# One stage in place of three ahead of the RWKV solve: sums over time on TensorE, two products on GpSimd

## The chip, the cores and the metric

One core of a Trainium2 chip runs the whole program. Times are device microseconds of that core; the metric is the time of one execution, and the median of three is given. The engines are TensorE (PE in the profile), VectorE (DVE), ScalarE (ACT), GpSimd (POOL) and SyncE (SP), which issues transfers.

## The reference

A model block with dilated attention beside a bidirectional RWKV-7 mixer, then a layer of retrieved experts, then a second block of four layers. What matters here is how the mixer prepares its recurrence, for 256 tokens and 8 heads of 64:

```python
zr = token_shift(z[..., 3 * A:], mu_prev, mu_next)      # r, k, v (512 each), xw, xa (64), xg (128)
g = jax.nn.sigmoid(xg) @ g_up
kk = hs(k * k_k)
kk = kk * lax.rsqrt(jnp.maximum(jnp.sum(kk * kk, axis=-1, keepdims=True), 1e-12))
for direction in range(2):
    w = -jax.nn.softplus(-(w_decay0[direction] + jnp.tanh(xw) @ w_decay_up[direction])) - 0.5
    decay = jnp.exp(-jnp.exp(w))
    a = jax.nn.sigmoid(a_gate0[direction] + xa @ a_gate_up[direction])
    k_dir = k * (1.0 + (a - 1.0) * k_a)
    ys.append(wkv7_scan(hs(r), hs(decay), hs(k_dir), hs(v), kk, hs(a), reverse=(direction == 1)))
# wkv7_scan: S_t = S_{t-1}(diag(w_t) - kk_t^T (a_t*kk_t)) + v_t^T k_t,  y_t = S_t r_t
```

The logarithm of the decay is `-exp(-0.5) * sigmoid(...)`, so decays over a stretch of tokens are exponentials of sums over time.

## The kernel before

Activations lie with features on the partitions: `zT[:, i, :]` is 128 features by 256 tokens. `rT`, `kT`, `vT` are four such tiles each; `zT[:, 20]` holds `xw` (partitions 0 to 63) and `xa` (64 to 127), `zT[:, 21]` holds `xg`. The program is a row of stages. In each, every engine has its own list of instructions, written out by hand, and waits on semaphores; a stage ends when all engines have ended it, and the next one begins some 0.3 us later. PSUM is `ps`, eight banks of 512 columns. All products here are in float32, which the trace shows as two passes for each.

The recurrence is solved in chunks of 128 tokens by matrix products (the stage that begins with line 1805). It needs, for each direction d, four factors (`alpha`, `beta`, `kappa`, `rho`), and `v`, `beta`, `kappa` turned so that tokens are on the partitions (`v_tok`, `bk_tok`). Three stages make them:

- Stage 1 (lines 1522 to 1565): TensorE multiplies `lora` by `zT[:, 20]`, 64 rows for the decay (line 1549) and the other 64 for the gate (1551). ScalarE takes tanh, then sigmoids with the bias in the instruction (`logw`, `aa`). TensorE also goes through the last eight of 32 tiles of a modulation matrix (`late_rows`, 464), which SyncE loads into a ring of six slots in `alpha`, `beta` and `kappa` (`late_load`, 429): six in the attention stage before, two here, when slots are free.
- Stage 2 (1567 to 1685): VectorE sums `logw` over time with 16 scans (1638), takes the sum at the chunk's middle off (1648), and makes the sum without the token's own term (1653). ScalarE takes three exponentials for each direction (1621 to 1623). VectorE scales `kk` (1659), makes the bonus (1663 to 1668), and multiplies ten times over 128x1024 (1671 to 1677).
- Stage 3 (1689 to 1716): TensorE turns six chunks (1700), VectorE and ScalarE copy three each.

The weights of later layers come through a ring of six slots, in order, refilled when a slot is used.

Of the kernel before, what the change touches and what calls it, by code (L numbers as in the profile page):

```python
# [30 lines left out]
P = 128  # L31
S = 256
# [20 lines left out]
ADA_LATE, LATE_RING = 32, 6  # L53
# [7 lines left out]
for _name, _n in (("c", 8), ("ada_b", 48), ("norm1_g", 8), ("mu_prev", 14), ("mu_next", 14), ("w_decay0", 8), ("a_gate0", 8),  # L61
                  ("k_k", 4), ("k_a", 4), ("r_k", 4), ("lnx_g", 4), ("lnx_b", 4), ("norm2_g", 8), ("q_norm_g", 1),
                  ("k_norm_g", 1), ("norm_w", 48), ("final", 8), ("pool_scale", 4), ("s5_d", 4), ("lam_re", S5T),
                  ("lam_im", S5T), ("log_dt", S5T)):
    VEC[_name] = (_at, _at + _n)
    _at += _n
# [79 lines left out]
def build(nc, A):  # L146

    with ExitStack() as ctx:
# [273 lines left out]
        late_in = [sem(f"late_in{i}") for i in range(LATE_RING)]  # L422
        late_used = sem("late_used")

        def late_load(sp, i):

            if i >= LATE_RING:
                sp.wait_ge(late_used, i - LATE_RING + 1)
            sp.dma_start(late_slot(i), A["ada_late"][i]).then_inc(late_in[i % LATE_RING], 16)
# [27 lines left out]
        def late_rows(pe, pair, bank):  # L457

            for n in range(2):
                i = 2 * pair + n  # L460
                pe.wait_ge(late_in[i % LATE_RING], 16 * (i // LATE_RING + 1))
# [691 lines left out]
        def attention(pairs, out, tag, late_of=None):  # L1153
# [25 lines left out]
            with ExitStack() as tmp, stage() as (block, (scored, shifted, maxed, exped, probs_ready, turned, turned_back,  # L1179
                                                         mixed, out_copied, lowered, v, *_)):  # L1180
                DEEP = 3
                if late_of:
                    @block.sync
                    def _(sp):
                        for i in late_of:
                            late_load(sp, i)
# [173 lines left out]
        def late_slot(i):  # L1360

            slot = i % LATE_RING
            return (alpha, beta, kappa)[slot // 2][:, slot % 2].rearrange("p a t -> p (a t)")
# [3 lines left out]
        lora_in = sem("lora_in")  # L1367
        attn = ExitStack()
# [132 lines left out]
        def head(tensor, i):  # L1501
# [5 lines left out]
                   for j in range(4)], mix, "dilated", range(LATE_PREP, LATE_PREP + LATE_RING))  # L1507
# [6 lines left out]

        feat = ExitStack()
        g_up = sb("g_up", [P, 512], where=feat)
        logw = sb("logw", [P, 2, 4, S], where=feat)
# [4 lines left out]
        with stage() as (block, (up_in, squashed, raised, sig_done, v, *_)):  # L1522
            @block.sync
            def _(sp):
                sp.dma_start(g_up[:, :], A["g_up"]).then_inc(up_in, 16)
                for i in range(LATE_PREP + LATE_RING, ADA_LATE):
                    late_load(sp, i)

            @block.scalar
            def _(act):  # L1530
                nc.scalar.activation(zT[0:64, 20, :], zT[0:64, 20, :], ACT.Tanh).then_inc(squashed, 1)
                nc.scalar.activation(zT[:, 21, :], zT[:, 21, :], ACT.Sigmoid).then_inc(squashed, 1)
                for d in range(2):
                    act.wait_ge(raised, 8 * d + 8)
                    for j in range(4):
                        bank, col = 4 * d + j // 2, j % 2 * S
                        nc.scalar.activation(logw[:, d, j, :], ps[:, bank, col:col + S], ACT.Sigmoid,
                                             bias=vec("w_decay0", 4 * d + j)).then_inc(sig_done, 1)
                        nc.scalar.activation(aa[:, d, j, :], ps[:, bank + 2, col:col + S], ACT.Sigmoid,
                                             bias=vec("a_gate0", 4 * d + j)).then_inc(sig_done, 1)  # L1540

            @block.tensor
            def _(pe):
                pe.wait_ge(lora_in, 16)
                pe.wait_ge(squashed, 1)
                for d in range(2):
                    for j in range(4):
                        bank, col = 4 * d + j // 2, j % 2 * S
                        nc.tensor.matmul(ps[:, bank, col:col + S], lora[0:64, d, j * P:(j + 1) * P], zT[0:64, 20, :],
                                         start=True, stop=True).then_inc(raised, 1)  # L1550
# [1966 lines left out]
```

## Time and profile before

| what | us |
|---|---|
| median of three runs | 2083.81 (2081.59 to 2084.3) |
| the profiled execution | 2085.11 |
| its span | 2083.2 |
| TensorE busy | 1839.3 (88%) |
| VectorE busy | 1488.5 (71%) |
| ScalarE busy | 1007.0 (48%) |
| GpSimd busy | 455.2 (22%) |

The shares are averages over the whole program. The change touches the stretch from 165.5 to 217.4 us, and the rows below are of that stretch and its borders. The clock column is the share of TensorE's full clock that was granted.

### The profile page before, as it was taken

How to read it: one execution, taken by the hardware profiler on the slowest of the kernel's cores; microseconds unless marked ns; L12 is line 12 of the kernel's file. 1: busy time of each engine (PE TensorE's matmuls, PEld its weight loads, DVE VectorE, ACT ScalarE, POOL GpSimd, SP SyncE). 2: the span in 40 equal slices, each digit the busy share in tenths (PEclk: the TensorE clock that was granted, in tenths of full speed). 3: DMA queues.
4: the chain of work that ended last, by engine and by line, in shares of the span. 5: the costliest groups of instructions: out<-in, count | busy, mean ns of one | idle time of the engine just before them, and what ended most of it. 6: DMA issues, size and time to landing. Idle time of an engine off the chain costs nothing. (4 is left out here: it accounts for less than half of the span.)

```text
span 2083.2 us, 33313 instructions
## 1 busy us (share of the span) xinstructions
PE 1839.3 (88%) x12202; PEld 1376.2 (66%) x12202; DVE 1488.5 (71%) x2602; ACT 1007.0 (48%) x2038; POOL 455.2 (22%) x463
## 2 busy tenths in 40 slices
PE   5974899988888777887789999889999999989998
PEld 4842887744443222222259999769998899968997
DVE  7666664787776776776567667877678887887666
ACT  3445212564444445444355555466556555546554
POOL 1010220144454433444410001002123331110000
PEclk8987999899999999999999999799999999999999
DMA  8870000499999999999965556125556556425553
GB/s 329 290 265 26 3 3 29 152 420 421 421 421 422 421 421 421 421 419 421 421 249 191 191 192 240 51 73 184 188 184 226 178 185 186 137 93 181 190 186 97
DMA packets 102973, 497.23 MB, mean 239 GB/s; under 512 B 11856, under 2 KB 16208, under 8 KB 69712
## 3 DMA queue, kind: packets, MB, share of 16 engines
q1 hardware_dynamic: 65312, 226.68, 32.4%
q0 software_dynamic: 36864, 268.45, 31.0%
q8 instruction: 67, 1.10, 0.2%
q10 hardware_dynamic: 688, 0.65, 0.1%
q14 instruction: 42, 0.34, 0.0%
HBM read 494.69 MB, written 1.05 MB: 238 GB/s over the span
## 5 line engine op out<-in xcount | busy, mean ns | idle before, releaser
L253 PE MATMUL ps<-srcs,wh 128*128 128x512 f32 x2000 | 711.7, 397 | 6.3 <-DVE srcs L267 3.4
L2267 PE MATMUL ps<-row,diag 128*128 128x512 f32 x1024 | 495.7, 619 | 118.9 <-ACT diag L2379 118.7
L255 PE MATMUL ps<-srcs,wl 128*128 128x256 f32 x2000 | 563.2, 282 | 0.0
L235 DVE TENSOR_TENSOR wl<-ring,wh 128x1024 fp32r<-128x1024 f32 x362 | 459.1, 1273 | 92.7 <-ACT wh L229 91.5
L2267 PEld LDWEIGHTS ps<-row,diag 128*128 128x128 f32 x1024 | 181.3, 192 | 421.1 <-ACT diag L2379 269.6
L2486 DVE CUSTOM_DVE_ANT_0 row<-row,h_tok 128x1024 f32<-128x1024 f32 x256 | 313.3, 1224 | 191.5 <-DMA row<-in_peer_uv,experts 181.4
L253 PEld LDWEIGHTS ps<-srcs,wh 128*128 128x128 f32 x2000 | 376.8, 188 | 93.3 <-issue 7.6
L229 ACT ACTIVATE wh<-ring 128x1024 fp32r<-128x1024 f32 x362 | 378.8, 1052 | 69.8 <-PE ps L255 43.7
L255 PEld LDWEIGHTS ps<-srcs,wl 128*128 128x128 f32 x2000 | 379.4, 190 | 2.5 <-issue 2.4
L2178 POOL DMA_INDIRECT row<-in_peer_uv,experts x256 | 280.4, 1095 | 386.2 <-PE ps L2267 345.5
L2372 ACT ACTIVATE acts<-dots 128x1 f32<-128x1 f32 x256 | 51.8, 202 | 329.8 <-DVE dots L2486 329.1
L245 PE MATMUL ps<-hidh,wh 128*128 128x256 f32 x704 | 198.0, 281 | 1.2 <-DVE wl L235 1.2
L245 PE MATMUL ps<-hidl,wh 128*128 128x256 f32 x704 | 197.4, 280 | 0.0
L245 PE MATMUL ps<-hidh,wl 128*128 128x256 f32 x704 | 197.3, 280 | 0.0
L245 PEld LDWEIGHTS ps<-hidh,wh 128*128 128x128 f32 x704 | 133.1, 189 | 5.6 <-DVE wl L235 2.4
L245 PEld LDWEIGHTS ps<-hidh,wl 128*128 128x128 f32 x704 | 133.3, 189 | 0.0
L245 PEld LDWEIGHTS ps<-hidl,wh 128*128 128x128 f32 x704 | 133.2, 189 | 0.0
L918 ACT ACTIVATE low_part<-ps 128x512 f32<-128x512 f32 x88 | 52.6, 597 | 124.4 <-PE ps L255 124.4
L980 DVE TENSOR_TENSOR gu<-ps,low_part 128x512 f32<-128x512 f32 x88 | 60.8, 691 | 67.7 <-ACT low_part L918 66.8
L2379 ACT ACTIVATE diag<-mats,weights 128x128 f32<-128x128 f32 x256 | 102.8, 401 | 8.4
L779 POOL TENSOR_TENSOR hT<-sq 128x512 f32<-128x512 f32 x6 | 9.2, 1532 | 440.3 <-ACT sq L771 440.3
L934 ACT ACTIVATE hidh<-hid 128x256 fp32r<-128x256 f32 x88 | 36.8, 418 | 111.5 <-DVE hid L993 109.2
(558 smaller groups left out, 2228.8 us busy)
## 6 DMA issues: line engine op xcount, KB each, us to landing
ring<-in_stream SPq DMA_DIRECT2D x378, 512.0 KB, 3.6
alpha<-in_ada_late SPq DMA_DIRECT2D x12, 512.0 KB, 5.5
beta<-in_ada_late SPq DMA_DIRECT2D x10, 512.0 KB, 5.9
kappa<-in_ada_late SPq DMA_DIRECT2D x10, 512.0 KB, 6.5
row<-in_peer_uv,experts POOLq DMA_INDIRECT x256, 15.3
bias<-in_attn_bias SPq DMA_DIRECT2D x8, 256.0 KB, 7.4
w<-in_cmp_w SPq DMA_DIRECT2D x1, 2048.0 KB, 7.4
mats<-in_mats SPq DMA_DIRECT2D x1, 1216.0 KB, 6.7
```

Source lines behind the costliest of these rows:

```text
L229: nc.scalar.activation(wh[:, n % PAIRS, :], ring[:, tile % RING, :], ACT.Copy).then_inc(high_done, 1)
L235: nc.vector.tensor_tensor(wl[:, n % PAIRS, :], ring[:, tile % RING, :], wh[:, n % PAIRS, :].bitcast(F32), ALU.subtract).then_inc(tiles_fre ...
L245: last = nc.tensor.matmul(out, left, right, start=(start and p == 0), stop=(stop and p == 2), skip_group_check=True)
L253: nc.tensor.matmul(out, wh[:, n, cols], source.rearrange("p a t -> p (a t)"), start=start, stop=stop, skip_group_check=True)
L255: return nc.tensor.matmul(out[:, 0:S], wl[:, n, cols], source[:, 0, :], start=False, stop=stop, skip_group_check=True)
L918: nc.scalar.activation(low_part[:, j % 2], ps[:, pair_of(j):pair_of(j) + 2, S:2 * S], ACT.Copy).then_inc(low_copied, 1)
L980: nc.vector.tensor_tensor(gu[:, j % 2], ps[:, pair_of(j):pair_of(j) + 2, 0:S], low_part[:, j % 2], ALU.add).then_inc(up_ready, 1)
L2178: pool.indirect_dma_start(out=row[:, s % ROWS, :], out_offset=None, in_=A["peer_uv"], in_offset=bass.IndirectOffsetOnAxis(ap=experts[:, t, ...
L2267: last = nc.tensor.matmul(y_part(t, half), diag[:, s % DIAGS, :], row[:, s % ROWS, D + half * 512:D + (half + 1) * 512], start=(slot == 0) ...
L2372: nc.scalar.activation(acts[:, s:s + 1], dots[:, s:s + 1], ACT.Gelu).then_inc(gelued, 1)
L2379: nc.scalar.activation(diag[:, s % DIAGS, :], mat("ident"), ACT.Copy, scale=weights[:, s:s + 1]).then_inc(diag_ready, 1)
L2486: nc.vector.tensor_tensor_reduce(u_row, u_row, h_tok[:, s // SLOTS, :], 1.0, 0.0, ALU.mult, ALU.add, dots[:, s:s + 1]).then_inc(dotted, 1)
```

## The change

The three stages become one. Its parts:

- The decay products are turned round: `zT[0:64, 20]` is now the stationary side and `lora` the moving one, so tokens are on the partitions and 512 features in the columns. Their bias, which then lies along the columns, is a product of a row of ones with `decay_row`, ahead of each. The gate products stay as they were.
- The sums over time are products of `logw` with a constant matrix `prefix` (128x256): its first half gives the sum up to and with the token, the second half without it, both less the sum of the first 64 tokens. They stay in PSUM, and the exponentials read them there. Scans, centrings and differences are gone.
- The affine step for `kd` of direction 1 is VectorE's. `kk` is scaled by one product over 1024 columns.
- GpSimd multiplies `rho` and `alpha` of direction 0. The other factors stay with VectorE.
- Turns of `v`, `kappa` and `beta` follow in the same stage, all copied by ScalarE, behind its exponential of the carry.
- All eight late tiles are loaded in the attention stage, six in the ring's slots and two in `rho`, behind three new or moved transfers (`decay_row`, `prefix`, `g_up`).

The core of the diff:

```diff
+        def late_arrival(i):
+            last = i - (ADA_LATE - LATE_MORE)
+            return (late_in[LATE_RING + last], 16) if last >= 0 else (late_in[i % LATE_RING], 16 * (i // LATE_RING + 1))
...
+        def load_features(sp):
+            sp.dma_start(decay_row[0:1, :, :].rearrange("p a t -> p (a t)"), A["decay_row"]).then_inc(lora_in, 16)
+            sp.dma_start(prefix, A["prefix"]).then_inc(lora_in, 16)
+            sp.dma_start(g_up, A["g_up"]).then_inc(lora_in, 16)
+            for i in range(LATE_PREP, ADA_LATE):
+                late_load(sp, i)
...
+                def decay_bias(d, c):
+                    nc.tensor.matmul(ps[:, W_BANK[d] + c, :], mat("ones")[0:1, :],
+                                     decay_row[0:1, 2 * d:2 * d + 2, :].rearrange(flat), start=True, stop=False,
+                                     skip_group_check=True)
+                def decay_product(d, c):
+                    nc.tensor.matmul(ps[:, W_BANK[d] + c, :], zT[0:64, 20, c * P:(c + 1) * P], lora[0:64, d, :],
+                                     start=False, stop=True, skip_group_check=True).then_inc(raised_w, 1)
+                def prefix_sums(d):
+                    for j in range(4):
+                        for c in range(TT):
+                            last = nc.tensor.matmul(ps[:, CUM_BANK + j, c * S:(c + 1) * S],
+                                                    logw[:, d, c, j * P:(j + 1) * P], prefix, start=True, stop=True)
+                    last.then_inc(cum_done, 1)
...
+                pe.wait_ge(exps, 3)
+                pe.wait_ge(ends_in, 1)
+                prefix_sums(1)
...
+                for n, (d, i) in enumerate(jobs):
+                    if n < 2:
+                        pe.wait_ge(v_copied, n + 1)
+                    else:
+                        pe.wait_ge(exps, 6)
+                        pe.wait_ge(ends_in, 2)
+                    pe.wait_ge(made, n + 1)
+                    turn_chunk(JOB_BANK[n], (beta, kappa)[i][:, d], d).then_inc(bk_turned, 1)
...
+                    nc.scalar.activation(chunks(inv2[:, d]), own, ACT.Exp, scale=sign).then_inc(exps, 1)
+                    if d == 0:
+                        act.wait_ge(late_used, ADA_LATE)
+                    nc.scalar.activation(chunks(rho[:, d]), own, ACT.Exp, scale=-sign).then_inc(exps, 1)
...
+                act.wait_ge(carry_in, 2)
                 nc.scalar.activation(carry[:, :, :], carry[:, :, :], ACT.Exp, scale=-DECAY)
+                for c in range(TT):
+                    act.wait_ge(v_turned, c + 1)
+                    nc.scalar.activation(v_tok[:, c, :], ps[:, (0, 7)[c], :], ACT.Copy).then_inc(v_copied, 1)
+                for n, (d, i) in enumerate(jobs):
+                    act.wait_ge(bk_turned, n + 1)
+                    nc.scalar.activation(bk_tok[:, d, i, :], ps[:, JOB_BANK[n], :], ACT.Copy)
+
+            @block.gpsimd
+            def _(pool):
+                pool.wait_ge(exps, 2)
+                nc.gpsimd.tensor_tensor(rho[:, 0], rho[:, 0], rT, ALU.mult)
+                pool.wait_ge(exps, 3)
+                pool.wait_ge(kk_scaled, 1)
+                nc.gpsimd.tensor_tensor(alpha[:, 0], alpha[:, 0], kk[:, :, :], ALU.mult)
...
+                scaled_by_decay(0)
                 dve.wait_ge(late_turned, 1)
                 late_mod(3).then_inc(mod_in, 1)
+                scaled_by_decay(1)
+                for d in range(2):
+                    carry_over(d)
...
-                    for j in range(4):
-                        for c in range(2):
-                            cols = slice(c * P, c * P + P)
-                            nc.vector.tensor_tensor_scan(cum[:, d, j, cols], mat("ones"), logw[:, d, j, cols], 0.0,
-                                                         ALU.mult, ALU.add).then_inc(v, n.one())
...
-                    nc.vector.tensor_tensor(chunks, chunks, mid[:, d, :].unsqueeze(2).broadcast_to([P, 8, P]),
-                                            ALU.subtract).then_inc(v, n.one())
```

TensorE before, from the first late rows to the last turn (`zT` is v in the turns; `mix` holds the modulation's column weights):

```order
L464 MATMUL ps<-alpha,mix 32x512 x4
L464 MATMUL ps<-beta,mix 32x512 x4
L464 MATMUL ps<-kappa,mix 32x512 x4
L464 MATMUL ps<-alpha,mix 32x512 x4
L196 UNCONDITIONAL_BRANCH
L1583 UNCONDITIONAL_BRANCH
L1586 MATMUL ps<-sq,mats 32x256 x4
L1590 MATMUL ps<-zT,g_up 128x256 x4
L1594 MATMUL ps<-sq,mats 128x256 x4
L473 MATMUL ps<-mats,ysum 128x2 x4
L1601 MATMUL ps<-sq,mats 128x512 x2
```

TensorE of the changed kernel from the sums over time of direction 0 to the bonus sums (`mix,logw` are the sums over time, `zT,mix` the gate products, `gT` in the row above them the decay bias):

```order
L1571 MATMUL ps<-gT,mats 128x512
L1576 MATMUL ps<-bonus,zT 128x512
L1582 MATMUL ps<-mix,logw 128x256 x8
L470 MATMUL ps<-alpha,mix 32x512 x4
L470 MATMUL ps<-beta,mix 32x512 x4
L470 MATMUL ps<-kappa,mix 32x512 x4
L470 MATMUL ps<-rho,mix 32x512 x4
L1621 MATMUL ps<-sq,mats 128x256 x4
L1582 MATMUL ps<-mix,logw 128x256 x8
L1629 MATMUL ps<-zT,mix 128x256 x4
L479 MATMUL ps<-mats,ysum 128x2 x4
L1588 MATMUL ps<-mats,zT 128x128 x8
```

The late rows moved behind the first sums over time, their last pair reads `rho`, and no boundary between stages stands in the row any more.

VectorE before, from the scaling of `kk` to the bonus:

```order
L1668 SCALAR_TENSOR_TENSOR sq<-sq,half_rk,zT 128x256 x4
L1671 TENSOR_TENSOR beta<-kk,aa 128x1024
L1673 TENSOR_TENSOR kappa<-vtok,hT 128x1024
L1674 TENSOR_TENSOR alpha<-alpha,kk 128x1024
L1675 TENSOR_TENSOR rho<-rho,zT 128x1024
L1677 TENSOR_TENSOR beta<-beta,hT 128x1024
L1671 TENSOR_TENSOR beta<-kk,aa 128x1024
L1673 TENSOR_TENSOR kappa<-sq,hT 128x1024
L1674 TENSOR_TENSOR alpha<-alpha,kk 128x1024
L1675 TENSOR_TENSOR rho<-rho,zT 128x1024
L1677 TENSOR_TENSOR beta<-beta,hT 128x1024
L480 TENSOR_TENSOR mod<-ps,vecs 128x8
```

VectorE of the changed kernel over the same work (`hT` holds the second exponential, `zT` as an input of `kappa` is `kd`):

```order
L1748 RECIPROCAL sq<-sq 128x256
L1750 TENSOR_TENSOR kk<-kk,ps 128x1024
L1755 TENSOR_TENSOR beta<-kk,aa 128x1024 x2
L1715 TENSOR_TENSOR kappa<-zT,hT 128x1024
L1717 TENSOR_TENSOR beta<-beta,hT 128x1024
L486 TENSOR_TENSOR mod<-ps,vecs 128x8
L1715 TENSOR_TENSOR kappa<-zT,hT 128x1024
L1717 TENSOR_TENSOR beta<-beta,hT 128x1024
L1720 TENSOR_TENSOR rho<-rho,zT 128x1024
L1722 TENSOR_TENSOR alpha<-alpha,kk 128x1024
L1710 TENSOR_TENSOR carry<-ends 128x4 x2
```

Two products over 128x1024 left VectorE (they are GpSimd's two), the modulation's addition moved between the two directions, and the bonus multiplications moved ahead of the scaling of `kk`.

## Rows read from the trace of the kernel before

**Rows 1.** Stretches by engine: busy us and instructions, then granted clock, DMA share, GB/s.
```profile
165.50:177.50 12.00, 9.28 (x64) 4.32 (x64) 2.57 (x7) 8.07 (x19) 0.00 (x0) 0.93 0.32 112
177.50:211.00 33.50, 8.70 (x36) 4.33 (x36) 31.72 (x49) 14.29 (x20) 0.00 (x0) 0.60 0.00 0
211.00:217.40 6.40, 5.36 (x24) 4.98 (x24) 2.08 (x3) 1.79 (x3) 0.00 (x0) 0.56 0.00 0
217.40:220.40 3.00, 2.96 (x72) 2.68 (x76) 2.16 (x7) 1.71 (x4) 0.47 (x1) 1.00 0.03 8
```

**Rows 2.** Timeline of TensorE: start, us, line, tiles, count, idle before and its releaser.
```profile
161.54 1.09 PE L1222 MATMUL ps<-mats,sc_dilated 128*128 128x128 f32 x8
...
166.15 0.45 PE L1549 MATMUL ps<-zT,bonus 64*128 64x256 f32 x1 [1.27 <-ACT zT L1531]
...
169.50 0.38 PE L1551 MATMUL ps<-zT,bonus 64*128 64x256 f32 x1
...
170.70 1.04 PE L464 MATMUL ps<-beta,mix 128*32 128x512 f32 x8
171.56 1.04 PE L464 MATMUL ps<-kappa,mix 128*32 128x512 f32 x8
174.19 1.05 PE L464 MATMUL ps<-alpha,mix 128*32 128x512 f32 x4 [1.59 <-DMA alpha<-in_ada_late]
...
211.16 1.94 PE L1700 MATMUL ps<-mats,zT 128*128 128x128 f32 x8 [9.29 <-PEq L196]
...
217.44 1.16 PE L1805 MATMUL ps<-alpha,beta 64*128 64x128 f32 x16 [0.93 <-PEq L196]
```

**Rows 3.** Timeline of ScalarE over the same stretch.
```profile
162.29 1.08 ACT L1333 ACTIVATE sq<-ps 128x512 f32<-128x512 f32 x2 [0.68 <-PE ps L1222]
...
166.03 1.28 ACT L1532 ACT_TABLE_LOAD   x1
...
173.20 0.57 ACT L1537 ACTIVATE logw<-ps,vecs 128x256 f32<-128x256 f32 x1
173.56 0.58 ACT L1539 ACTIVATE aa<-ps,vecs 128x256 f32<-128x256 f32 x1
...
180.05 2.06 ACT L1611 ACTIVATE vtok<-aa,omka,vecs 128x256 f32<-128x256 f32 x4
...
186.29 1.06 ACT L1621 ACTIVATE rho<-zT 128x1024 f32<-128x1024 f32 x1
187.26 1.04 ACT L1622 ACTIVATE hT<-zT 128x1024 f32<-128x1024 f32 x1
...
216.55 0.60 ACT L1716 ACTIVATE bk_tok<-ps 128x512 f32<-128x512 f32 x1 [1.11 <-PE ps L1700]
```

**Rows 4.** Timeline of VectorE in the second stage.
```profile
179.13 2.62 DVE L1638 TENSOR_TENSOR_SCAN zT<-mats,logw 128x128 f32<-128x128 f32 x8
181.67 1.72 DVE L1642 RECIPROCAL sq<-sq 128x256 f32<-128x256 f32 x1
...
196.35 1.67 DVE L1668 SCALAR_TENSOR_TENSOR sq<-sq,half_rk,zT 128x256 f32<-128x256 f32 x4
...
199.08 1.22 DVE L1673 TENSOR_TENSOR kappa<-vtok,hT 128x1024 f32<-128x1024 f32 x1
200.21 1.22 DVE L1674 TENSOR_TENSOR alpha<-alpha,kk 128x1024 f32<-128x1024 f32 x1
```

**Rows 5.** Timeline of GpSimd and VectorE in the solve.
```profile
221.65 1.28 POOL L1914 TENSOR_TENSOR lower<-zT,mats 128x512 f32<-128x512 f32 x1 [0.45 <-ACT zT L1889]
221.67 1.80 DVE L1949 TENSOR_TENSOR mix<-zT,mats 128x512 f32<-128x512 f32 x1
...
225.07 0.68 DVE L1949 TENSOR_TENSOR mix<-zT,mats 128x512 f32<-128x512 f32 x1
...
232.71 2.50 POOL L1914 TENSOR_TENSOR lower<-zT,mats 128x512 f32<-128x512 f32 x2 [4.62 <-PE ps L1773]
...
234.69 0.69 DVE L1930 TENSOR_TENSOR hT<-ps,mats 128x512 f32<-128x512 f32 x1 [1.81 <-PE ps L1787]
```

More of the change, by code:

```diff
@@ L1151, in even_projection, with attention @@
             return Part(sync, scalar, tensor, vector, gpsimd, None, sums_to)
-        def attention(pairs, out, tag, late_of=None):
+        def attention(pairs, out, tag, loads=None):
             NP = len(pairs)
@@ L1658, in _, with carry_over @@
-                dve.wait_ge(spread, 1)
-                nc.vector.tensor_tensor(kk[:, 0:3, :], kk[:, 0:3, :], ps[:, 4:7, 0:S], ALU.mult).then_inc(v, n.one())
-                nc.vector.tensor_tensor(kk[:, 3, :], kk[:, 3, :], spread_out(3), ALU.mult).then_inc(v, n.one())
-                for d in range(2):
-                    dve.wait_ge(kd_in, 4 * d + 4)
-                    nc.vector.tensor_tensor(kd[d], kd[d], kT, ALU.mult).then_inc(v, n.one())
+                def carry_over(d):
+                    dve.wait_ge(ends_in, d + 1)
+                    nc.vector.tensor_tensor(carry[:, d, :], ends[:, d, :, 0], ends[:, d, :, 1], ALU.subtract
+                                            ).then_inc(carry_in, 1)
@@ new lines, in scaled_by_decay @@
+                def scaled_by_decay(d):
+                    dve.wait_ge(exps, 3 * d + 1)
+                    nc.vector.tensor_tensor(kappa[:, d], kd[d], inv2[:, d], ALU.mult).then_inc(made, 1)
+                    dve.wait_ge(v, n.now)
+                    nc.vector.tensor_tensor(beta[:, d], beta[:, d], inv2[:, d], ALU.mult).then_inc(made, 1)
+                    if d:
+                        dve.wait_ge(exps, 3 * d + 2)
+                        nc.vector.tensor_tensor(rho[:, d], rho[:, d], rT, ALU.mult)
+                        dve.wait_ge(exps, 3 * d + 3)
+                        nc.vector.tensor_tensor(alpha[:, d], alpha[:, d], kk[:, :, :], ALU.mult)
@@ new lines, in _ @@
+                for j in range(4):
+                    nc.vector.tensor_scalar(kk[:, j, :], kT[:, j, :], vec("k_k", j), None, ALU.mult).then_inc(v, n.one())
+                nc.vector.tensor_scalar(omka[:, :], vec_all("k_a"), -1.0, 1.0, ALU.mult, ALU.add).then_inc(omka_ready, 1)
+                dve.wait_ge(v, n.now)
+                nc.vector.tensor_tensor(sq[:, 0:4, :], kk[:, :, :], kk[:, :, :], ALU.mult).then_inc(sq_ready, 1)
+                nc.vector.tensor_scalar(half_rk[:, :], vec_all("r_k"), 0.5, None, ALU.mult).then_inc(v, n.one())
@@ new lines, in _ @@
+                dve.wait_ge(summed, 1)
+                nc.vector.tensor_scalar(kk_root_at, ps[:, 7, S:2 * S], 1e-12, None, ALU.max).then_inc(kk_ready, 1)
+                dve.wait_ge(omka_ready, 1)
+                for j in range(4):
+                    dve.wait_ge(sig_a, 4 + j + 1)
+                    nc.vector.tensor_scalar(kd[1][:, j, :], aa[:, 1, j, :], vec("k_a", j), omka[:, j:j + 1], ALU.mult,
+                                            ALU.add).then_inc(v, n.one())
+                dve.wait_ge(v, n.now)
```

282 lines of the change are left out of this document (134 added, 148 removed).

## The prediction

> **What bounds the kernel now.** I read the split of the stretch by stage first, since the change touches 52 of 2083 us and shares of the whole span say nothing of it. In [rows 1] the reader is to see three stages: 12 us in which TensorE is busy for 9.3, 33.5 us in which VectorE is busy for 31.7 and TensorE for 8.7, and 6.4 us in which TensorE is busy for 5.4. So the first is set by products and sigmoids, the second by VectorE alone, the third by transpositions. Then the engines' timelines. TensorE [rows 2] begins the low-rank products at 166.15, after a wait for the tanh, runs them until 169.9, later waits 1.59 us for a late tile of the modulation matrix, and starts the solve (the next stage) at 217.44. The solve cannot start before all six transpositions are copied, and nothing else holds it. What follows is fed by a ring of weight tiles that is full: no bytes move from 177.5 to 217.4 [rows 1]. I therefore take what the stretch gains to reach the end of the span.
>
> The sum is made on the profiled execution (2085.11 us, span 2083.2). The median of the other runs, 2083.81, is 1.3 lower, and I take the gain off that.
>
> **The change, part by part.** One stage replaces three. I lay its work out on the clock of the trace before, from 165.6, one tanh of 0.4 ahead of the table load at 166.03 [rows 3].
>
> TensorE, first half. One pass of a 64-row product over 256 columns comes every 0.215 us: the two row halves have 16 passes each between 166.15 and 169.50 plus the last, side by side [rows 2]. A product is two passes, so 0.43 us for 256 columns and 0.86 for 512. Eight gate products (rows 64 to 127) make 3.44 us; beside them, in rows 0 to 63, stand two bias products and two decay products of 512 columns, 3.44 us too. All overlapped would be 3.44, all one after the other 6.9. As they are issued (two gates, then one wide) the wide one starts with the second gate, and each half takes 2.15: I take 4.3, to 169.9, near the overlapped end because the only such pair in the trace overlaps fully. The sums of squares (four products into different quarters, half a late pair of the 0.86 below, and 0.2 until the result is there) 0.6, to 170.6. Four wide products of the second direction, all in the same rows: 4 x 0.86 = 3.4, to 174.0. The sums over time, which replace VectorE's scans: 8 products of 256 columns, 3.4, to 177.5. The late rows: in [rows 2] a pair comes every 0.86 us (four quarter products, 8 passes of 0.43, four at a time), so four pairs take 3.5, to 181.0; that the tiles are now loaded in the attention stage removes the wait of 1.59, and nothing reads them earlier. Spreading the inverse root is of the size of the sums of squares, 0.6, and 0.3 for the wait on its own first half: 181.9.
>
> ScalarE: tanh, a table load of 1.28 and eight sigmoids of 0.36 from start to start [rows 3] end at 170.2; four affine steps 2.0 [rows 3], 172.2; two sigmoids over 512 by 173.3, the last one only when TensorE is through, 174.8. Sigmoid, table load, root, table load (0.4 + 1.28 + 0.4 + 1.28) end at 178.2, the first exponential at 179.2. The next one writes rho, which now holds two late tiles, so it waits for the late rows at 181.0: rho and alpha at 0.97 each [rows 3], then the small copy, 183.3. TensorE's second sums wait for that copy: 183.4 to 186.9. Behind them on TensorE stand the gate products, the turn of the modulation row and the first turn of v, to 190.2. ScalarE's second three exponentials end at 190.0.
>
> VectorE loses 16 scans, the two centrings and the two differences (scans 2 x 2.62 [rows 4], and four steps of the size that comes every 1.14 there). Its early work (root, bonus with four steps in 1.67, reciprocal of 1.72 [rows 4]) ends by 179.8, before the spread, and is hidden. Then the scaling of kk, 1.24, to 183.2. Then two products for beta, kappa and beta of direction 0 at 1.14 from start to start [rows 4], 4.6. Beside this GpSimd multiplies rho and alpha, each 128x1024. Two of 128x512 took 2.50 there [rows 5], so I take 2.5 for each of ours (no row has the size; the ends are 1.2, VectorE's own, and 3.6, if each half is held up as VectorE's 1.80 was).
>
> Is GpSimd's work free? In [rows 5] VectorE's 128x512 product with both inputs in SBUF took 0.68 alone and 1.80 when GpSimd's began at 221.65, 0.02 earlier; the one with an input in PSUM took 0.69 under GpSimd's work. All four of VectorE's products here have both inputs in SBUF. So they line up: rho on GpSimd 182.2 to 184.7, then 4.6 + 2.5 = 7.1, to 191.8. Had VectorE kept both, it would be through at 183.2 + 6 x 1.14 = 190.0. Moved to GpSimd they cost 1.8 more, not 2.3 less. The Trainium skill speaks against this part too: "SBUF — State Buffer", section "SBUF: two separate sides", has the shared port pair as a lock held for a whole instruction, the loser blocked; and "GPSIMD Engine Reference", section "Engine selection", has two-input work about twice as slow there. By that the sum is as above, and the trace agrees (1.12 us more for an overlap of 1.28).
>
> After it: the modulation's addition 0.2, four products of direction 1 (4.6), two small differences 0.3: 196.9. Only now can ScalarE take the exponential of the carry, and behind that instruction on ScalarE are queued the two copies of v and the four of beta and kappa. TensorE's last four turns wait for the copies of v, the solve for all. With copies 0.5 apart (two in 1.08, [rows 3]) the tail is 0.2 + 1.1 + 0.4 + 1.5 + 0.6 = 3.8 if turns take 0.43 us (eight in 1.09 at the higher clock, [rows 2]), and 5.3 if they take 0.86 (1.94 for eight at the lower). The gate copy, the bonus sums (1.7) and their product lie beside it. Half way, 4.6: 201.5, and 0.3 for the boundary between stages, as from 217.15 to 217.44: 201.8. The old start was 217.44, so 15.6 us less. For a solve that may start at the lower clock I take off 0.3: **15.3 us, 2068.5**.
>
> Costed at nothing: three more transfers queued ahead of the late tiles in the attention stage (the tiles behind them are first read at 177.5, 12 us after the stage begins; without that cover TensorE would wait for the last of them, as it did 1.59 us for one), two boundaries gone (in the sum already), vecs eight columns narrower.
>
> **The clock.** TensorE is granted 0.93 of full speed in the first stage, where it is busy for three quarters, 0.60 in the second, where it is busy for a quarter, 0.56 through the turns, and 1.00 when the solve starts [rows 1]. The new stage has it busy about 25 of 36 us, with gaps only behind 182 us. So I take the higher clock (2.4 GHz) until then and either of the two in the tail.
>
> **The rivals.**
> A, GpSimd beside VectorE for free: then VectorE is through by 187.8 and waits for the turn of the modulation row at about 190.0, so 1.8 earlier: 2066.7; with a fast tail 2066. For it only the row with an input in PSUM; against it the 1.80.
> B, the first products do not overlap, since a bias product has one row and another tile shape than any in the trace: 6.9 in place of 4.3 delays all behind: 2.6 more, 2071.1.
> C, the clock falls for part of the stage. TensorE's work on the path at full speed is 4.3 + 0.6 + 3.4 + 3.4 + 3.5 + 0.9 = 16.1, another 3.4 for the second sums, up to 1.5 in the tail and 3 in the first of the solve. A third of it at the lower clock costs 8: 2076.
> D, slower than before: the same place, with TensorE at the lower clock (1.2 GHz) from start to end, as in the second stage of [rows 1]. That adds 16.1 + 3.4 + 1.5 + 3 = 24, so 9 slower: 2092. It decides from about 16 us of such work at half speed. Against it: at 166 us the clock is granted in full, and the work after that is denser than before.
> E, it shortens the stretch but the span does not follow, because a later part is set by transfers that run on their own: 2083.8. Against it: no byte moves while the stretch runs.
>
> **How the numbers follow.** My line (13 to 17.5 us) 0.57, A 0.14, B 0.13, C 0.11, D 0.02, E 0.03. The likeliest is 2068.5. The range from 2063.5 (A, with GpSimd at its low end and the fast tail) to 2075.5 (B, with a slow tail and half of C) leaves out the rest of C, D and E and a little below. What can be told from no change is about 0.2%, 4.2 us. Faster is all but D and E: 0.95; same 0.03; slower 0.02.
>
> **What would show it.** Right: the solve starts at 200.5 to 203.5; the longest row of VectorE waits from 183 to 192 is not a wait but products of 2 us and more in place of 1.2 while GpSimd is busy; no wait for a late tile; the last thing before the solve is ScalarE's copies, behind a wait for the carry. Wrong: bias and gate passes that do not overlap; a granted clock below 1 between 166 and 182; products of VectorE at 1.2 us beside GpSimd's; a rest of the program whose length from the solve's start to the end differs from 1866 us (2083.2 - 217.4) by more than 2.

## The result, and the profile after

| | median us (lowest to highest, runs) |
|---|---|
| before | 2083.15 (2080.32 to 2086.88, 14) |
| after | 2087.55 (2080.94 to 2094.8, 14) |
| after over before | 1.0022 (95%: 1.0012 to 1.0031) |
| predicted | 2068.5 (2063.5 to 2075.5) |

The change makes the kernel slower by 0.2%, where the prediction had it 0.7% faster. The profiled execution of the changed kernel took 2082.77 us (span 2081.0), one of its quicker ones, and the profiled one of the kernel before (2085.11) one of its slower ones. So two questions are open: why the profile shows 2.2 us of gain in the span and not 15.3, and why the median shows none.

**The stage.** From the tanh to the first product of the solve it takes 43.5 us (166.27 to 209.81) where the old three took 51.8 (165.6 to 217.44). The prediction had 36.2. TensorE's timeline of the changed kernel (start, us, line, tiles, count of passes, idle before with its releaser) answers to [rows 2]:

```profile
166.29 1.10 PE L1566 MATMUL ps<-zT,bonus 64*128 64x256 f32 x4 [0.73 <-PEq L196]
167.32 1.12 PE L1571 MATMUL ps<-gT,mats 1*128 1x512 f32 x2
168.37 1.13 PE L1566 MATMUL ps<-zT,bonus 64*128 64x256 f32 x4
169.43 1.24 PE L1571 MATMUL ps<-gT,mats 1*128 1x512 f32 x2
170.60 0.79 PE L1566 MATMUL ps<-zT,bonus 64*128 64x256 f32 x1
170.61 1.22 PE L1576 MATMUL ps<-bonus,zT 64*128 64x512 f32 x1
...
174.12 0.64 PE L1604 MATMUL ps<-sq,mats 128*32 128x256 f32 x8
174.69 1.12 PE L1571 MATMUL ps<-gT,mats 1*128 1x512 f32 x2
175.74 1.12 PE L1576 MATMUL ps<-bonus,zT 64*128 64x512 f32 x2
176.79 1.78 PE L1571 MATMUL ps<-gT,mats 1*128 1x512 f32 x2
178.50 2.07 PE L1576 MATMUL ps<-bonus,zT 64*128 64x512 f32 x2
180.50 5.41 PE L1582 MATMUL ps<-mix,logw 128*128 128x256 f32 x16
185.84 1.06 PE L470 MATMUL ps<-alpha,mix 128*32 128x512 f32 x8
...
189.41 1.50 PE L1621 MATMUL ps<-sq,mats 32*128 32x256 f32 x8
191.70 3.69 PE L1582 MATMUL ps<-mix,logw 128*128 128x256 f32 x16 [0.80 <-ACT ends L1681]
...
205.20 1.12 PE L1588 MATMUL ps<-mats,kappa 128*128 128x128 f32 x4 [3.04 <-ACT vtok L1691]
...
209.81 2.08 PE L1852 MATMUL ps<-alpha,beta 64*128 64x128 f32 x16 [0.93 <-PEq L196]
```

Gates (L1566, rows 64 to 127) and bias products (L1571, one row) follow each other at 1.05 us, one group starting where the other is done; gates and decay products (L1576, rows 0 to 63) interleave from 170.60 on. A pass of 512 columns takes 0.43 up to 170.3 and 0.86 from there to 173.7. There is no wait for a late tile (L470 at 185.84 follows at once), where [rows 2] had 1.59 us.

The stretches of the same kernel answer to [rows 1], with its columns; the granted clock stands behind the last bracket:

```profile
166.30:170.30 4.00, 4.00 (x12) 1.88 (x12) 2.56 (x7) 3.27 (x6) 0.00 (x0) 1.00 0.00 2
170.30:173.70 3.40, 3.40 (x12) 2.60 (x12) 0.00 (x0) 0.91 (x3) 0.00 (x0) 0.50 0.00 0
173.70:177.10 3.40, 3.40 (x16) 1.04 (x14) 2.24 (x6) 2.95 (x7) 0.00 (x0) 1.00 0.01 2
177.10:183.90 6.80, 6.80 (x12) 3.27 (x11) 5.36 (x8) 4.54 (x8) 0.00 (x0) 0.50 0.01 2
183.90:204.00 20.10, 15.98 (x93) 9.89 (x92) 14.04 (x11) 8.01 (x11) 5.65 (x2) 1.00 0.00 0
204.00:210.00 6.00, 3.87 (x18) 3.50 (x20) 1.75 (x6) 3.57 (x7) 0.00 (x0) 0.54 0.00 0
```

In the first four TensorE has no idle time at all, and yet the clock stands at half (1.2 of 2.4 GHz) in the second and the fourth: 10.2 us, each behind a group of one-row and 64-row products. In the last, at half too, TensorE had waited 3 us for ScalarE.

VectorE and then GpSimd and ScalarE of the same kernel, to be read beside [rows 4], [rows 5] and [rows 3]:

```profile
190.98 1.22 DVE L1750 TENSOR_TENSOR kk<-kk,ps 128x1024 f32<-128x1024 f32 x1 [5.96 <-PE ps L1621]
192.31 5.08 DVE L1755 TENSOR_TENSOR beta<-kk,aa 128x1024 f32<-128x1024 f32 x2
197.31 1.21 DVE L1715 TENSOR_TENSOR kappa<-zT,hT 128x1024 f32<-128x1024 f32 x1
...
199.59 0.15 DVE L486 TENSOR_TENSOR mod<-ps,vecs 128x8 f32<-128x8 f32 x1
```

```profile
190.66 2.35 POOL L1699 TENSOR_TENSOR rho<-rho,zT 128x1024 f32<-128x1024 f32 x1 [57.09 <-ACT rho L1678]
192.98 3.33 POOL L1702 TENSOR_TENSOR alpha<-alpha,kk 128x1024 f32<-128x1024 f32 x1
```

```profile
204.46 0.21 ACT L1688 ACTIVATE carry<-carry 128x8 f32<-128x8 f32 x1 [5.18 <-DVE carry L1710]
204.57 1.06 ACT L1691 ACTIVATE vtok<-ps 128x512 f32<-128x512 f32 x2
206.36 0.60 ACT L1694 ACTIVATE bk_tok<-ps 128x512 f32<-128x512 f32 x1 [0.72 <-PE ps L1588]
...
208.92 0.60 ACT L1694 ACTIVATE bk_tok<-ps 128x512 f32<-128x512 f32 x1 [0.26 <-PE ps L1588]
```

Two products of VectorE that come 1.14 apart elsewhere take 5.08 together beside GpSimd's. And the copies of v stand on ScalarE behind 5.18 us of waiting for the carry.

**The rest.** If each instruction of VectorE is set beside the same one of the kernel before, the changed kernel is 7.6 us ahead at 210 us, where the solve begins, and some 8.0 ahead all the way from 400 to 1084, through the gathers (GpSimd's 256 indirect transfers of expert rows). Then it loses: 5.1 ahead at 1315, 4.9 at 1710, 2.2 at the end. From the last gather's issue to the end it is 1033.0 us before and 1038.7 after. In that part most of TensorE's time is in pairs of streamed products, L253 over 512 columns and L255 over 256, which no edit touches. The costliest group of the page (busy us, mean ns of one), of the kernel before and of the changed one:

```profile
L253 PE MATMUL ps<-srcs,wh 128*128 128x512 f32 x2000 | 711.7, 397 | 6.3 <-DVE srcs L267 3.4
```

```profile
L253 PE MATMUL ps<-srcs,wh 128*128 128x512 f32 x2000 | 719.6, 402 | 6.9 <-DVE srcs L267 3.4
```

Waits for operands are about the same (6.3 and 6.9 us); the products themselves are 5 ns longer. Pairs that follow each other without a wait come every 348.5 ns before and every 352.1 after. So the prediction's last sign of being wrong has come: the rest, from the solve's start to the end, is 1871.2 us and not 1866.

### The profile page after: what moved, and what is told of

It is laid out like the page before. It is cut to its first block and busy times, and to the rows that moved or that the text cites. A ratio compares the mean times of both kernels' runs of the same rounds, so it can differ in the third digit from the quotient of the medians.

```text
span 2081.0 us, 33339 instructions
## 1 busy us (share of the span) xinstructions
PE 1865.7 (90%) x12234; PEld 1390.2 (67%) x12234; DVE 1478.0 (71%) x2577; ACT 1005.9 (48%) x2035; POOL 464.1 (22%) x465
## 3 DMA queue, kind: packets, MB, share of 16 engines
HBM read 494.83 MB, written 1.05 MB: 238 GB/s over the span
## 5 line engine op out<-in xcount | busy, mean ns | idle before, releaser
L253 PE MATMUL ps<-srcs,wh 128*128 128x512 f32 x2000 | 719.6, 402 | 6.9 <-DVE srcs L267 3.4
L255 PE MATMUL ps<-srcs,wl 128*128 128x256 f32 x2000 | 562.5, 281 | 0.0
L253 PEld LDWEIGHTS ps<-srcs,wh 128*128 128x128 f32 x2000 | 377.3, 189 | 101.8 <-issue 7.6
L255 PEld LDWEIGHTS ps<-srcs,wl 128*128 128x128 f32 x2000 | 379.7, 190 | 2.5 <-issue 2.4
L2419 ACT ACTIVATE acts<-dots 128x1 f32<-128x1 f32 x256 | 51.8, 202 | 326.5 <-DVE dots L2533 325.8
```

The source lines that it names most:

```text
L253: nc.tensor.matmul(out, wh[:, n, cols], source.rearrange("p a t -> p (a t)"), start=start, stop=stop, skip_group_check=True)
L255: return nc.tensor.matmul(out[:, 0:S], wl[:, n, cols], source[:, 0, :], start=False, stop=stop, skip_group_check=True)
L2419: nc.scalar.activation(acts[:, s:s + 1], dots[:, s:s + 1], ACT.Gelu).then_inc(gelued, 1)
```

## The experiments

Two theories for the rest. L: the vector block (`vecs`) that lost eight columns moved everything allocated behind it in SBUF by 32 bytes, and the streamed products run slower there. R: whatever time the stage gains is given back later, since something else paces the rest (the prediction's E). Each experiment was timed in turn with the kernel before, and a ratio is to it, with its 95% interval. "The stage" is always the time from the tanh to the first product of the solve, and it and the products' means are of the one profiled execution.

**e1_again.** The changed kernel, no edit, beside the next three on one chip.

> The changed kernel once more, nothing edited. In its first profile the solve starts at 209.8 us and VectorE is 8 us ahead of the kernel before from 500 to 1084 us; then the streamed feed-forward layers lose 6 of it, because a pair of products (512 and 256 columns) takes 352.1 ns on the mean in place of 348.5. Theory 1 (the pace is drawn anew in each execution): the solve starts within 2 us of 209.8 again, and the mean pair is another number between 347 and 354; the times spread over 8 us or more as before (2081 to 2095). Theory 2 (the pace belongs to the program, by its code or its addresses): the pair is 352 again in about the same places, and the ratio to the kernel before is 1.002 again.

2084.17 us (2078.6 to 2095.41), ratio 1.0014 (0.9997 to 1.003). The result holds within its interval: no gain. A slow pair of products belongs to the program, then, and is not drawn anew in each execution. L253's mean is 401 ns again, last gather to end 1039.9.

**e2_vecs250.** Eight columns that nothing reads, where w_decay0 had stood.

```diff
-("mu_next", 14), ("a_gate0", 8),
+("mu_next", 14), ("unused", 8), ("a_gate0", 8),
```

> The changed kernel with eight unused columns put back into vecs, which is 250 wide again, so that every tensor behind it stands at its old address within a partition (the width went to 242, 32 bytes less). Theory 2 with addresses as the cause: the pair of products is back at 348, the time at 2083.2 less 8, near 2075. Theory 1, or code rather than addresses: no difference from the changed kernel, 2083 to 2090.

2076.49 us (2070.73 to 2084.61), ratio 0.9975 (0.9962 to 0.9988). Some 8 us less than e1 for data that is never read. The stage is not shorter (45.0), so the gain is in the rest: last gather to end is 1034.7, 5.2 less than in e1's profile, and on its page

```profile
L253 PE MATMUL ps<-srcs,wh 128*128 128x512 f32 x2000 | 708.8, 396 | 6.6 <-DVE srcs L267 3.4
```

**e3_before_vecs258.** The kernel before, with eight unused columns more, at the end of the block.

```diff
-("lam_im", S5T), ("log_dt", S5T)):
+("lam_im", S5T), ("log_dt", S5T), ("unused", 8)):
```

> The kernel before with eight unused columns added at the end of vecs (258 wide), so that the tensors behind it stand at the same place modulo 64 bytes as in the changed kernel. Theory 2 with addresses as the cause: the pair goes from 348.5 to 352 and the time to 2083 plus 6 to 12. Theory 1 or code: 2083 within 2, pair anywhere from 347 to 354.

2082.7 us, ratio 1.0004 (0.9994 to 1.0015): no change. So neither a larger block nor a shift by 32 bytes upward costs time by itself; the changed kernel's shift is downward.

**e4_delay.** The changed kernel, with two reciprocals (1024 and 768 columns) added at the end of VectorE's list in the stage, which makes the stage 9 us longer.

```diff
+                nc.vector.reciprocal(aa[:, 0], aa[:, 0])
+                nc.vector.reciprocal(aa[:, 1, 0:3], aa[:, 1, 0:3])
```

> The changed kernel with two reciprocals over 1024 and 768 columns of a tensor that nobody reads any more, at the end of VectorE's list in the new stage, about 12 us behind 205.6. The solve then starts near 217.5, as before the change. If what the stretch gains is passed on: 8 us slower than the changed kernel, 2095. If time gained there is taken back by something with a clock of its own (a transfer, a fixed phase): within 2 of the changed kernel, 2087. If the changed kernel is merely unlucky in where its later stages fall against the clock's changes: at or below 2087, in spite of the delay.

2095.61 us (2093.09 to 2098.42), ratio 1.0071 (1.0057 to 1.0084). The stage is 52.6 us in place of 43.2, and the time 11 more than e1's. A delay is passed on in full. That what is gained is passed on too is seen in e9, below. Nothing else paces the rest: R falls.

**e5_gap32.** The changed kernel, its block still narrow, with 32 unused bytes behind it. This parts the place in SBUF from the block's load (250 columns are one transfer's size, too).

```diff
+        gap = sb("gap", [P, 8])
```

> The changed kernel, vecs still 242 wide, with an unused tensor of eight columns between vecs and mats: all tensors behind it are 32 bytes further up, at their addresses of the kernel before; vecs itself, its columns and its source in HBM stay as changed. e2 (vecs 250 wide) gained 8 to 11 us over the changed kernel. If the place in SBUF of what lies behind vecs is what costs: as e2, 2076 to 2078, and 1033 to 1036 us from the last gather to the end. If it is the columns within vecs, or its source's size: as the changed kernel, 2084 to 2088, and 1038 to 1042 us there.

2076.58 us (2073.41 to 2086.78), ratio 0.9981 (0.9966 to 0.9996), the streamed products at 397 ns. It is the place. Nor is it the clock: over its executions the mean granted clock is 0.9646, over those of the changed kernel 0.9647. And from the last gather to the end e1's profile has 45.5 us at half the clock and e2's 55.5, and yet e2's is the shorter.

**e6_rows128.** e2, with the bias products over 128 rows: the bias in row 0 and zeros in the rest. For the stage the theories are: K, one-row products let the clock fall; or the clock falls whatever their rows.

```diff
-nc.tensor.matmul(ps[:, W_BANK[d] + c, :], mat("ones")[0:1, :],
-                 decay_row[0:1, 2 * d:2 * d + 2, :].rearrange(flat), ...
+nc.tensor.matmul(ps[:, W_BANK[d] + c, :], mat("ones"),
+                 decay_row[:, 2 * d:2 * d + 2, :].rearrange(flat), ...
```

> On e2: the bias product uses all 128 rows of the array (the bias in the first row, zeros in the others) in place of one row. Length and count of the products are unchanged. Theory of the clock (TensorE's clock fell at 168.7 and 178.9 us, each time behind products over 1 and 64 rows, though the engine never paused): the granted clock stays at 1.0 through the first 15 us of the stage, the stage gets 4 to 5 us shorter, 2072. Rival (the clock falls for another reason, as the little work in the attention before): clock and stage as in e2 (45.0 us), 2076.5 within 2. The gate products may also cease to run at 1.05 us a pair: no effect is expected, they do not overlap the bias either way.

2071.92 us (2070.51 to 2076.93), ratio 0.9953 (0.994 to 0.9965); the stage is 38.0 us, 7.0 less than e2's and 5.5 less than the changed kernel's; the time is 4.6 less than e2's. More arithmetic in the same passes makes it shorter. Its TensorE timeline and its stretches:

```profile
165.52 1.10 PE L1566 MATMUL ps<-zT,bonus 64*128 64x256 f32 x4 [0.73 <-PEq L196]
166.55 1.12 PE L1571 MATMUL ps<-gT,mats 128*128 128x512 f32 x2
...
171.75 0.64 PE L1604 MATMUL ps<-sq,mats 128*32 128x256 f32 x8
172.32 1.12 PE L1571 MATMUL ps<-gT,mats 128*128 128x512 f32 x2
...
176.53 3.72 PE L1582 MATMUL ps<-mix,logw 128*128 128x256 f32 x16
```

```profile
165.60:176.50 10.90, 10.90 (x40) 4.62 (x40) 6.51 (x14) 8.37 (x17) 0.00 (x0) 1.00 0.01 2
176.50:199.50 23.00, 17.73 (x101) 11.43 (x100) 18.70 (x21) 11.95 (x18) 5.66 (x2) 1.00 0.00 1
199.50:203.50 4.00, 3.04 (x16) 2.58 (x17) 0.48 (x1) 2.88 (x5) 0.00 (x0) 0.61 0.00 0
```

The order and the 1.05 us steps are as before, and the clock stays at 1.00 until TensorE waits for ScalarE.

One profile with 128 rows would prove little, but all of them agree. In each of the eight profiles with one-row products (the changed kernel, e1, e2, e4, e5, e7, e8, e12) the clock falls to half within the first 5 us of the stage, with TensorE busy, and stands there for 10.2 us in all (the changed kernel, e1, e12), 13.7 (e2, e4, e5, e8) or 20.5 (e7) before the late rows are through. In neither of the two with 128 rows (this one and e9) does it fall there. The 3.4 us more of it in e2 fit its stage, which is 1.5 us longer than the changed kernel's.

**e7_vector.** e2, with VectorE doing rho and alpha of direction 0, and nothing on GpSimd.

```diff
-                nc.gpsimd.tensor_tensor(rho[:, 0], rho[:, 0], rT, ALU.mult)
-                nc.gpsimd.tensor_tensor(alpha[:, 0], alpha[:, 0], kk[:, :, :], ALU.mult)
-                    if d:
+                    # for both d
```

> On e2: VectorE does rho and alpha of direction 0 itself, GpSimd nothing. VectorE and GpSimd, by the first trace, took 6.9 us from kk's end at 192.3 to 199.6 for four products and two. Six at 1.14 are 6.8. Theory of the forecast (they line up for SBUF, at 2.5 each for GpSimd): stage 0.3 to 2 us shorter. Rival (GpSimd's work is free): 2.3 longer. In time: 2076.5 within 2, not to be told from e2; the trace decides.

2074.67 us (2072.28 to 2076.4), ratio 0.9956 (0.9943 to 0.9969). VectorE's timeline:

```profile
193.43 1.22 DVE L1741 TENSOR_TENSOR kk<-kk,ps 128x1024 f32<-128x1024 f32 x1 [5.76 <-PE ps L1621]
194.75 2.36 DVE L1746 TENSOR_TENSOR beta<-kk,aa 128x1024 f32<-128x1024 f32 x2
...
201.57 0.16 DVE L486 TENSOR_TENSOR mod<-ps,vecs 128x8 f32<-128x8 f32 x1
```

Six products take 6.82 us (194.75 to 201.57), where four beside GpSimd's took 7.28 (192.31 to 199.59). The work that was moved to GpSimd costs 0.46 us more there than on VectorE. The medians of e2 and e7 are 1.8 apart with intervals that overlap, so the timed runs bear out the sign no better than weakly. In this one profile the clock was low through the first half, so the whole stage came out longer than e2's:

```profile
165.70:186.20 20.50, 20.50 (x42) 8.96 (x42) 8.12 (x15) 9.72 (x20) 0.00 (x0) 0.50 0.00 1
```

TensorE was busy for every bit of those 20.5 us. So how long the clock stays down behind such products differs between executions. This stage, of 47.6 us, is the nearest to rival D that was seen.

**e8_tail.** e2, with the exponential of the carry put last on ScalarE, behind the copies of v, beta and kappa.

```diff
-                act.wait_ge(carry_in, 2)
-                nc.scalar.activation(carry[:, :, :], carry[:, :, :], ACT.Exp, scale=-DECAY)
                 ... copies of v, beta and kappa
+                act.wait_ge(carry_in, 2)
+                nc.scalar.activation(carry[:, :, :], carry[:, :, :], ACT.Exp, scale=-DECAY)
```

> On e2: ScalarE takes the exponential of the carry last, behind the copies of v, beta and kappa, which then need not wait for VectorE's last products. In the first trace the copies ran from 204.6 to 209.5, and VectorE ended at 205.6. If the tail is on the path: the stage ends with VectorE's bonus, 3.5 to 4 us earlier, 2072.5. Rival (the solve starts at the lower clock whenever it starts, and takes it back): stage 3.5 shorter, time within 1 of e2.

2072.76 us (2071.32 to 2078.75), ratio 0.9957 (0.9944 to 0.9969); the stage is 3.7 us shorter than e2's (41.3). ScalarE now copies v in time, with the carry behind:

```profile
198.97 0.64 ACT L1689 ACTIVATE vtok<-ps 128x512 f32<-128x512 f32 x1
200.34 0.60 ACT L1689 ACTIVATE vtok<-ps 128x512 f32<-128x512 f32 x1 [0.73 <-PE ps L1588]
202.49 2.07 ACT L1692 ACTIVATE bk_tok<-ps 128x512 f32<-128x512 f32 x4 [1.56 <-PE ps L1588]
204.42 0.23 ACT L1694 ACTIVATE carry<-carry 128x8 f32<-128x8 f32 x1
```

**e9_all.** e2 with the edits of e6, e7 and e8 together.

> On e2 (vecs 250 wide): the three edits of e6, e7 and e8 together: bias products over 128 rows, rho and alpha of direction 0 on VectorE, the carry's exponential last. Singly they gave 2071.9, 2074.7 and 2072.8 against 2076.5. If e6 and e8 act at different places: the stage gets 7.0 and 3.8 us shorter than 45.0, near 34.5, and the time 2068 within 2; the VectorE edit adds within 1 of nothing. Rival (what is taken off the stage ahead of the tail is waited for elsewhere): 2071 or more.

2065.02 us (2062.97 to 2065.66), ratio 0.9907 (0.9892 to 0.9921): faster than both kernels (four runs, 2.7 us apart), and 1 us below the band that was expected. The stage is 10.7 us shorter than e2's and the time 11.5 less, so a gain reaches the end. It takes 34.3 us, as expected, at a granted clock of 1.00 to its end (TensorE is busy for 4.0 of the last 6 us):

```profile
176.00:192.00 16.00, 14.18 (x90) 9.37 (x89) 11.77 (x14) 10.29 (x14) 0.00 (x0) 1.00 0.00 0
192.00:198.00 6.00, 3.98 (x27) 2.76 (x27) 5.62 (x9) 2.80 (x7) 0.00 (x0) 1.00 0.00 0
```

**e10_nobias.** e2 without the four bias products; w_decay0 is left out of the decay.

```diff
-                    decay_bias(0, c)
-                    decay_bias(1, c)
```

> On e2: the four bias products are left out, so w_decay0 is not added to the decay. It prices them. Theory (they overlap nothing and let the clock fall): stage as short as with e6's 38.0 us less 4 products of 1.05, so 34 to 35 us if the 64-row products alone keep the clock up; 2068. Rival (the clock falls with 64-row products alone): 39 to 41 us, 2073.

2068.35 us (2063.86 to 2070.8), ratio 0.9925 (0.9913 to 0.9937). TensorE's timeline:

```profile
162.30 2.18 PE L1566 MATMUL ps<-zT,bonus 64*128 64x256 f32 x9 [0.73 <-PEq L196]
164.11 0.69 PE L1576 MATMUL ps<-bonus,zT 64*128 64x512 f32 x1
164.32 0.59 PE L1566 MATMUL ps<-zT,bonus 64*128 64x256 f32 x2
...
166.03 0.64 PE L1603 MATMUL ps<-sq,mats 128*32 128x256 f32 x8
...
170.10 5.38 PE L1582 MATMUL ps<-mix,logw 128*128 128x256 f32 x16 [1.52 <-ACT logw L1666]
```

The first nine passes of the gates stand alone, and from 164.11 the decay products run beside the others, as they do in e6 (from 169.72). By the medians the four bias products cost 8.1 us in e2 and 3.6 in e6's form. By the profiles the stage is 37.1 us, which is 8.0 less than e2's and only 1.0 less than e6's; it lies between the theory's 34 to 35 and the rival's 39 to 41. The four steps of 1.05 are gone (4.2 us), but TensorE then waits 1.52 us for ScalarE's last sigmoid, and the sums over time take 5.38 us in place of 3.7, at half the clock for most of it. Before that fall TensorE came from 64-row products and from the wait, and which of the two counted this run doesn't tell.

**e11_before_gap96.** The kernel before, with 96 unused bytes ahead of the constant matrices. Together with the cut of 32 this is 128 bytes, so everything behind stands as in the changed kernel, but for whole steps of 128.

```diff
+        gap = sb("gap", [P, 24])
```

> The kernel before with an unused tensor of 24 columns (96 bytes) ahead of mats, so that what lies behind it stands where it does in the changed kernel modulo 128 bytes. A shift of 32 bytes down cost 8 to 10 us in the changed kernel (e5); the shift of 32 up in e3 cost nothing in time, though the mean pair went from 348.5 to 349.8 ns. Theory (it is the place modulo 128): the kernel before takes 6 to 10 us more, 2090, mean pair 352. Rival (it is the place itself, or it needs the changed kernel): 2083 within 2, mean pair below 350.

2090.17 us (2084.17 to 2095.0), ratio 1.0025 (1.0013 to 1.0037). The kernel before, untouched in every instruction, is slowed as the changed one is, by a place that e2 and e5 take away. The pairs come every 351.0 ns, and not the 352 that was expected:

```profile
L254 PE MATMUL ps<-srcs,wh 128*128 128x512 f32 x2000 | 717.9, 400 | 7.2 <-DVE srcs L268 3.4
```

**e12_gap64.** The changed kernel with 64 unused bytes at that place.

```diff
+        gap = sb("gap", [P, 16])
```

> The changed kernel with an unused tensor of 16 columns (64 bytes) ahead of mats: modulo 64 bytes all behind it stands as in the changed kernel, modulo 128 it stands as in e3. If 64 bytes are the period: as the changed kernel, 2084 to 2088, mean pair 352. If it is 128: as e3 against before, 2076 to 2078, mean pair 349 to 350.

2072.18 us (2070.79 to 2081.61), ratio 0.9954 (0.9937 to 0.9971). Its place is that of the changed kernel modulo 64 bytes, and it is fast, so the effect doesn't repeat every 64 bytes; -32 and +96 alike fit 128. It is 4.4 us below e2 and e5, with intervals that overlap. But its pairs of products come every 350.7 ns, the same as e11's, where 349 to 350 was expected for a fast one.

The runs by the place of what stands behind the vector block, beside the kernel before (the last columns are of the profiled execution):

| shift, bytes | kernel | ratio | L253, ns | last gather to end, us |
|---|---|---|---|---|
| 0 | before | 1 | 397 | 1033.0 |
| 0 | e2, e5 | 0.9975, 0.9981 | 396, 397 | 1034.7, 1035.4 |
| 0 | e6, e7, e8 | 0.9953, 0.9956, 0.9957 | 397, 397, 396 | 1031.1, 1030.2, 1031.9 |
| 0 | e9, e10 | 0.9907, 0.9925 | 396, 397 | 1035.0, 1035.3 |
| -32 | after, e1 | 1.0022, 1.0014 | 402, 401 | 1038.7, 1039.9 |
| -32 | e4 | 1.0071 | 402 | 1042.4 |
| +96 | e11 | 1.0025 | 400 | 1042.4 |
| +32 | e3, e12 | 1.0004, 0.9954 | 398, 399 | 1034.1, 1033.8 |

Where the time goes is seen best if VectorE's instructions behind the last gather are set one by one beside those of the kernel before. From 425 us behind the gather to the end, the four profiles at -32 and +96 lose 3.7 to 4.1 us, steadily. The seven experiments at 0 stay within -0.3 and 1.0. The two at +32 win 3.3 back, having lost 4.4 and 4.2 up to there. At -32 and +96, as at +32, one profile or more is of each of the two kernels.

## Why the prediction was wrong

**The step that failed** is the last phrase of "costed at nothing": vecs eight columns narrower. It is worth 8 us of the time (0.0039 of it between e1 and e2, 0.0041 between the changed kernel and e5), 14 against e12, and 5 to 6 on the kernel before alone (e11). Of the 19 us between the forecast and the median, the stage is 7.3 (43.5 for 36.2, below), this place 8, and the rest, some 3 us, is how much higher the changed kernel's first 14 runs came out than e1's 12. I looked for what the cut saves (a few columns of a load) and not for what it moves. That it acts through the place is shown by e2, e5, e11 and e12. That it acts on TensorE's streamed products is argued from the traces and not shown: 2000 of them, 4 to 5 ns longer, are 8 to 10 us, while the stretch that holds most of them is 5 to 6 us longer. And the mean does not tell a slow place from a fast one: pairs come every 351.0 ns in e11 and every 350.7 in e12, with 1042.4 and 1033.8 us from the last gather to the end. Which tensor behind the block has to stand where, and what in the chip makes 128 bytes matter, no run here tells.

**The stage**, term by term, in us (each rounded, so the columns add up within 0.1). The prediction's own steps against the changed kernel and e6:

| term | predicted | after | e6 |
|---|---|---|---|
| first products (gates, bias, decay) | 4.3 | 7.8 | 6.2 |
| sums of squares | 0.6 | 0.6 | 0.6 |
| four wide products, direction 1 | 3.4 | 5.8 | 4.2 |
| sums over time | 3.5 | 5.3 | 3.7 |
| late rows | 3.5 | 3.6 | 3.6 |
| spread, to kk scaled | 2.2 | 2.8 | 2.8 |
| VectorE's products | 13.7 | 12.2 | 12.2 |
| tail to the solve | 4.9 | 5.5 | 4.8 |
| sum | 36.2 | 43.5 | 38.0 |

- First products. Rival B was right in kind: bias and gates did not overlap. What I took as evidence, the overlap of gates and decay in [rows 2], was of two 64-row tiles; I wrote that a one-row tile is another shape and still took the overlapped end. Each change between the two groups costs 0.19 besides (steps of 1.05 for 0.86 of passes), in the direction-1 products as well, which the prediction had at 0.86 each. At full clock that is 1.9 + 0.8 in e6, 2.7 in all, where the rival had 2.6.
- The Trainium skill's "TensorE: Matmul & The Clock Gate", "Part 3: Packing small matmuls — row/col tiling", has products on different row groups of the array run at the same time. Gates and decay, two tiles of 64 rows, bear it out (170.60 and 170.61). Bias products in row 0 beside gates in rows 64 to 127 do not, though their row groups differ; the two tiles differ in height as well.
- The clock. The higher clock, because the only gaps lie behind 182 us, is the second reason that failed. There were no gaps up to there, and the clock fell twice. Rival C was right in kind, for 5.5 us of the stage (43.5 to 38.0) and by e6's edit, with the fall in eight profiles of eight with one-row products and in none of two without. I took a busy TensorE for a sufficient sign, and [rows 1] could not tell more, since the stretches with a low clock there were also idle ones. The same page, "Part 1: The HAM clock gate (the "warmup" mystery)", has the clock set by how busy TensorE has been. Taken as busy time the trace disagrees: 10.2 us at half clock in stretches that were busy from end to end.
- GpSimd. Right in direction: products of 2.54 us on average stood where the prediction had put them, and leaving the work on VectorE is shorter. Its size was 0.46 us, not 1.8: rho's 2.35 us began while VectorE scaled kk (190.66 and 190.98), and that product, with an input in PSUM, took its usual 1.22. The sum had put all of rho between VectorE's other products.
- The tail. Right in mechanism: the last thing before the solve was ScalarE's copies behind the carry, with turns at the lower clock. 5.5 us is the slow end that I had worked out (5.3) and averaged away.
- Late tiles, the boundaries and the ring: right, no wait appeared, and what the stage loses (e4) or gains (e9) reaches the end, so rival E falls.

Stage and place together: e2 has the changed stage at the old place and takes 2076.49, 8.0 above the forecast; e6, without the fall of the clock, 2071.92, inside the range and near rival B's 2071.1. The changed kernel also spreads more than the one before (14 us against 6.6). Its quicker runs are those of the higher mean clock, from 2080.94 us at 0.969 to 2094.8 at 0.962; the kernel before shows no such order (2080.15 at 0.960, 2085.61 at 0.967, in the rounds of e11).

## What to carry to other kernels

An edit that makes one tensor narrower moves all that is allocated behind it: hold the place with unused bytes before an edit is judged, and try two or three places once the rest is settled (here 32 bytes were worth 8 us, half of the gain that was forecast). Give TensorE's small products full rows of zeros where the passes stay the same, as this held the clock up here (5.5 us of the stage), and don't count two tile shapes as overlapping unless a row shows that very pair. When work goes in order on an engine, put an instruction that waits for the last result (here the carry's exponential) behind what others wait for.

## What the runs showed of the hardware

- Addresses: two kernels with the same instructions, the tensors 96 bytes further on in SBUF, 2083.72 and 2090.17 us; a streamed product of 512 columns 397 and 400 ns on average. Shifts of -32 and +96 bytes cost time and 0 and +32 do not, which fits a repeat every 128 bytes and rules out 64.
- The granted clock fell to half with TensorE busy for 100% of a stretch (170.30 to 173.70 and 177.10 to 183.90; 20.5 us on end in e7's profile), behind one-row and 64-row products. It fell in all eight profiles with one-row products and, with 128 rows in the place of one, in neither of two.
- A change between products of one row or 128 rows and those of 64 rows costs TensorE 0.19 us (steps of 1.05 for 0.86 of passes).
- GpSimd's product of 128x1024 took 2.35 us beside one of VectorE's with an input in PSUM, and 3.33 beside two with both in SBUF; those two took 5.08 in place of 2.36.
- Runs of the changed kernel differ with their mean granted clock: 2080.94 us at 0.969 and 2094.8 at 0.962. Those of the kernel before do not: 2080.15 at 0.960 and 2085.61 at 0.967.
